# Adding a gating bias with a one-row matmul of its own, and adding the attention part last

## The reference, cut to what matters

```python
def spatial_gating(u, v, tiny, ln_g, ln_b, w_s, b_s):
    b, s, _ = v.shape
    vn = layer_norm(v, ln_g, ln_b).reshape(b, s // CHUNK, CHUNK, SGU_GROUPS, SGU_GROUP_DIM)
    mixed = jnp.einsum("gpq,bnqgc->bnpgc", w_s, vn) + b_s.T[:, :, None]
    return u * (mixed.reshape(b, s, SGU_WIDTH) + tiny)

tiny = tiny_attention(tq, tk, tv, tk_c, tv_c) @ tiny_w_o     # tiny_w_o is 64 x 1024
o_a = spatial_gating(u, v, tiny, sgu_ln_g, sgu_ln_b, sgu_w_s, sgu_b_s)
```

## Time and profile before

| | before |
|---|---|
| median of 3 runs | 2415.87 us (2413.20 to 2421.04) |
| profiled execution, its own time | 2415.87 us |
| its span, first to last instruction | 2414.1 us |
| mean granted TensorE clock | 0.933 |
| TensorE busy | 2010.9 us, 83% of the span |
| TensorE's share of the chain that ended last | 68% |
| first projection matmul of the second layer starts | 806.65 us |
| transposes of the tiny attention's output start | 971.38 us |
| gating matmuls start | 973.32 us |
| first matmul of `pe_qkv` starts | 989.60 us |

### The profile page before, as it was taken

How to read it: one execution, slowest core, us unless ns; L and a number is a source line. 1 busy time by engine, 2 the same in 40 slices (tenths; PEclk the granted TensorE clock), 3 DMA queues, 4 the chain that set the end, 5 groups by cost and what they waited for, 6 DMA issues and landing times.

```text
span 2414.1 us, 33274 instructions
## 1 busy us (share of the span) xinstructions
PE 2010.9 (83%) x13566; PEld 1361.5 (56%) x13567; DVE 923.0 (38%) x2043; ACT 552.9 (23%) x1018; POOL 401.2 (17%) x379
## 2 busy tenths in 40 slices
PE   3899989688781698996776998987999998999875
PEld 2677778454341686784444665754555555555432
DVE  2144552532214225215766122224443444434325
ACT  2132412211112214114665110020111111111111
POOL 0000000222211000001100000001444545444320
PEclk8899999699996797899999999978999999999998
DMA  6654530689993212012110122214899999999967
GB/s 258 243 227 175 210 123 12 237 338 417 417 386 134 79 53 70 18 53 79 48 48 2 61 88 104 97 53 169 350 360 357 400 404 402 365 358 395 382 247 311
DMA packets 97403, 514.79 MB, mean 213 GB/s; under 512 B 25154, under 2 KB 26210, under 8 KB 43100
## 3 DMA queue, kind: packets, MB, share of 16 engines
q1 hardware_dynamic: 62592, 449.60, 47.2%
q0 software_dynamic: 29504, 51.31, 6.0%
q10 hardware_dynamic: 5148, 11.59, 1.4%
HBM read 508.87 MB, written 49.81 MB: 231 GB/s over the span
## 4 chain that ended last, share of the span: by engine, by line
PE 68%; DVE 10%; DMA 10%; ACT 7%; issue 3%; ACTq 1%; POOL 0%; SPq 0%; DVEq 0%; POOLq 0%
PE ps L249 29%; PE ps L1689 16%; PE ps L1756 8%; DMA arena<-in_egu 7%; PE ps L1655 2%; ACT arena L2773 2%; DVE arena L2809 2%; PE ps L402 2%; DMA arena<-in_ada 2%; PE ps L1743 1%; ACT arena L2784 1%; PE ps L2758 1%; DMA arena<-y_rows 1%; PE ps L424 1%; ACT arena L267 1%
## 5 line engine op out<-in xcount | busy, mean ns | idle before, releaser
L1689 PE MATMUL ps<-arena 128*64 128x256 f32 x4096 | 479.4, 388 | 54.0 <-DMA arena<-in_egu 35.9
L1689 PEld LDWEIGHTS ps<-arena 128*64 128x64 f32 x4096 | 301.4, 140 | 256.3 <-DMA arena<-in_egu 66.2
L249 PE MATMUL ps<-arena 128*128 128x256 f32 (+4 forms) x1276 | 323.4, 416 | 2.4 <-DVE arena L491 1.3
L249 PEld LDWEIGHTS ps<-arena 128*128 128x128 f32 (+1 forms) x1276 | 229.0, 203 | 92.7 <-issue 71.2
L1756 PE MATMUL ps<-arena 128*64 128x512 f32 x1024 | 243.4, 604 | 37.0 <-issue 29.1
L1637 POOL DMA_INDIRECT arena<-h_rows,arena x160 | 193.2, 1208 | 312.6 <-DVE arena L1618 162.6
L1643 POOL DMA_INDIRECT y_rows<-arena x160 | 160.2, 1002 | 419.2 <-DVE arena L1787 369.6
L1751 DVE COPY arena<-ps 128x256 f32<-128x256 f32 (+1 forms) x96 | 36.5, 380 | 431.9 <-PE ps L1743 431.9
L1730 ACT ACTIVATE arena<-ps 128x256 f32<-128x256 f32 (+1 forms) x96 | 33.4, 348 | 503.8 <-PE ps L1689 503.8
L300 DVE TENSOR_TENSOR wlb<-arena,whb 128x1024 fp32r<-128x1024 f32 (+1 forms) x46 | 55.7, 1213 | 242.1 <-ACT whb L292 242.1
L1756 PEld LDWEIGHTS ps<-arena 128*64 128x64 f32 x1024 | 67.7, 136 | 134.7 <-issue 131.0
(11 more groups left out here) (392 smaller groups left out, 3062.2 us busy)
## 6 DMA issues: line engine op xcount, KB each, us to landing
arena<-in_egu SPq DMA_DIRECT2D x204, 1024.0 KB, 12.4
arena<-in_ed SPq DMA_DIRECT2D x102, 1024.0 KB, 8.4
arena<-in_ada SPq DMA_DIRECT2D x48, 1024.0 KB, 7.1
arena<-in_win SPq DMA_DIRECT2D x33, 1024.0 KB, 4.9
arena<-y_rows SPq DMA_DIRECT2D x20, 1024.0 KB, 13.9
arena<-in_wout SPq DMA_DIRECT2D x8, 1024.0 KB, 6.8
arena<-in_nabias POOLq DMA_DIRECT2D x16, 512.0 KB, 3.9
h_rows<-arena ACTq DMA_DIRECT2D x8, 512.0 KB, 2.9
```

What stands on the lines that cost most here:

```text
L249: z = pe.matmul(o, l, r, start=start and i == 0, stop=stop and i == len(pairs) - 1, skip_group_check=check)
L1689: z = pe.matmul(b[64 * j:64 * j + 64, 256 * s:256 * s + 256], XV[:, c, 64 * h:64 * h + 64], wk(k)[:, j * 256:j * 256 + 256], start=k == 0, ...
```

## The change

The identity rows and rows 64 to 71 of `TQ` are gone. `b_s` is loaded once as one row of 4 KB into row 0 of `BSR`. In each group a matmul of one row by 512 columns (a row of ones times the group's part of `BSR`, read four times over) opens the bank, the four mixing matmuls follow, and the 64-row matmul on `TQ` comes last, so that the wait for `totT` stands in front of it.

```diff
-                    (cut(TQ[64:72, :], 4), bc(a["bs_row"].rearrange("o (g p) -> (o g) p", g=8).unsqueeze(1), [8, 4, 128]))]
+                    (BSR[0:1, :], a["bs_row"])]
             for i, (dst, src) in enumerate(late):
                 act.dma_start(dst, src).then_inc(*l2.up("late", "late", i, by=16))
-            act.activation(cut(TWO[64:72, :], 8), bc(ident[64:72, 64:72].unsqueeze(2), [8, 8, 128]), ACT.Copy).then_inc(
-                *l2.up("act", "eight"))
...
-                w.wait_ge(*l2.to("eight"))
+                pe.matmul(cut(b.ap, 4), ones[0:1, :], bc(BSR[0:1, cols].unsqueeze(1), [1, 4, 128]), start=True, stop=False,
+                          skip_group_check=True)
+                for n in range(4):
+                    pe.matmul(b.ap[:, n * 128:(n + 1) * 128], VN[:, n, cols], WST[:, cols], start=False, stop=False,
+                              skip_group_check=True)
                 w.wait_ge(*ta.to("totT"))
-                pe.matmul(b.ap, TWO[0:72, cols], TQ[0:72, :], start=True, stop=False, skip_group_check=True)
-                for n in range(4):
-                    z = pe.matmul(b.ap[:, n * 128:(n + 1) * 128], VN[:, n, cols], WST[:, cols], start=False, stop=n == 3,
-                                  skip_group_check=True)
-                z.then_inc(*sg.up("pe", "mm", g))
+                pe.matmul(b.ap, TWO[0:64, cols], TQ[0:64, :], start=False, stop=True, skip_group_check=True).then_inc(
+                    *sg.up("pe", "mm", g))
```

## The result

The changed kernel took 2454.09 us, the median of 4 runs (2446.53 to 2457.18), against 2415.95 us before, the median of 4 (2413.20 to 2421.04). The ratio is 1.0146, 95% interval 1.0128 to 1.0166: it is 1.5% slower. Forecast was slower, by 11 us; it is 38 us, more than three times that, and 21 us above the upper end of the range. The way was right, the size was not. The profiled execution has a span of 2447.5 us, and the mean granted clock fell from 0.933 to 0.924.

A forecast was written before the change was run, and what follows sets the result against it. TensorE was taken to bound the kernel at the gating. 11.0 us there (some 6 columns, 5 row-count changes, hole included) plus 0.3 for the transfer gave +11.3 us on 2415.87: 2427.2 us, 8-in-10 range 2420 to 2433.

The forecast's parts named there:

- The bound: At the gating, TensorE bounds the kernel, running without a gap into the projection, with one hole of 1.08 us.
- Columns: In the gating, eight added one-row matmul pairs cost 0.85 us each at full clock, 6.8 us for all.
- Changes of row count: In the gating, three changes per group, each about 0.2 us at full clock and 0.30 at the lower clock.
- The disputed third change: Between groups, the step from 64 rows to 1, absent from the trace: bounds 0 and 0.20 us, taken as 0.20.
- Two changes in a group: Rival at the gating: 64 rows to 1 is free; +9.7 us, 2425.6 us; chance 0.11.
- Columns only: Rival at the gating: changes of row count cost nothing; +6.8 us with the transfer, 2422.7 us; chance 0.10.
- The sum at the gating: Group 0 at lower clock, groups 1 to 7 at full clock, 3.19 us each; projection 11.0 us later.
- What the new order covers: Before `totT`, group 0's one-row and mixing matmuls fill TensorE's only hole, giving back at most 1.08 us.
- The transfer and the collision: Front of second layer: removing `b_s` packets gains 0.2 us at most; earlier weight load delays late loads; +0.3 us taken.
- The loads collide fully: Rival at the front: late loads end 1.0 us later, clock rises later too; +13 to +14 us, 2429.5; chance 0.09.
- The late loads did not give way: Rival at the front said they would: projection up to 4.15 us sooner, +6.9 us, 2422.7 us; chance 0.06.

The follow-up runs named there:

- both128: Changed kernel with bias and tiny-attention matmuls both on 128 rows, added rows zeros; stretch from last transpose to projection 21.7 us, ratio to before 1.0010.
- warm4: Changed kernel with bias and tiny-attention matmuls on 128 rows in the first four groups, last four unchanged; stretch 25.1 us, ratio to before 1.0010.
- narrow64: Kernel before with its 72-row matmul cut to 64 rows and `b_s` left out; stretch 32.8 us, ratio to before 1.0097.
- tiny72: Changed kernel with the last matmul of each group on 72 rows instead of 64, added rows zeros; stretch 26.4 us, ratio to before 1.0063.
- block64: Kernel before with 64 rows for 72, `b_s` left out, all eight 64-row matmuls ahead of all mixing; stretch 24.2 us, ratio to before 1.0057.
- batched: Changed kernel reordered: eight bias matmuls, then all mixing, then eight tiny-attention matmuls, a bank per group; stretch 30.7 us, ratio to before 1.0035.
- dummy128row: Kernel before with one more 128-row matmul of 16 columns of zeros in each group; stretch 31.8 us, ratio to before 1.0052.
- changes4: Changed kernel with 128-row bias matmul and the 64-row matmul cut in two, first half ahead of mixing; stretch 28.3 us, ratio to before 1.0103.
- the dummies: Kernel before with one more 16-column matmul of zeros per group, on 1, 64 or 128 rows; ratios to before 1.0063, 1.0074, 1.0052.
- order72: Kernel before with only the new order, mixing first, then the 72-row matmul, identity rows kept; stretch 14.9 us, ratio to before 0.9983.
- attn72_order: Kernel before with mixing first, 72-row matmul last, and the attention's score matmuls on 72 rows instead of 64; stretch 15.4 us, ratio to before 0.9983.
- tiny128: Changed kernel with the tiny-attention matmul on 128 rows, added rows zeros, bias matmul still one row; stretch 26.3 us, ratio to before 1.0037.
- after_again: Changed kernel run once more, unchanged, against the kernel before; stretch 48.2 us, ratio to before 1.014.
- bias128: Changed kernel with the bias matmul on 128 rows, added rows zeros, tiny-attention matmul still 64 rows; stretch 25.6 us, ratio to before 1.0035.

## Why the prediction was wrong, by its steps

**The bound: right.** The gating is on the path: of the 33.4 us by which the span grew, 30.8 are there.

**Columns: right in size at full clock.** 0.85 us a pair. In both128, where nothing but the columns is added, the stretch grew by 4.3 us; eight pairs of 0.85 are 6.8, and less the hole of 1.1 and 1.1 for a rise that comes 2.1 us sooner that is 4.6.

**Changes of row count: right in size and number.** Forecast were 0.20 us at full clock and 0.30 at the lower one, three to a group. At the lower clock the group of 6.00 us is 5.12 of columns and 3 x 0.29; at full clock warm4 has 3.19 us, to the digit. The disputed third change, from 64 rows to one, costs like the others: the two between 64 and 128 rows are 0.29 each in narrow64, and at full clock the group of tiny72, with two changes, takes 3.00 us against 3.19 with three. Thus "Two changes in a group" and "Columns only" fall, and the Trainium skill's rule, in "TensorEngine Tiling (Array Packing)", Key Properties, that a change of mode drains the engine, agrees with these rows for 64 to 1 row too.

**The step that failed: the clock.** The sum at the gating let the clock rise at about 978.0, as before: it put group 0 "at the lower clock" and "Groups 1 to 7 at full clock", and gave the rise 1.5 us either way. In the changed kernel all eight groups ran at 0.50. The rise was carried over from the kernel before as if it were a matter of time since TensorE became busy. It hung on what TensorE streams (tiny72: eight rows of zeros more in one matmul of three, and the clock rose in its profile). The stretch of 8 x 6.00 us is all my own lower-clock prices; only the clock in it was wrong, and that made +30.8 out of +11.0. Half-speed groups were priced in the prediction for group 0 alone, and no rival asked what it would cost if all eight stayed there: 8 x 6.0 = 48 us could have been reckoned from the earlier trace rows. The trace of the kernel before had a sign of it, too. Ahead of the gating, from 940.4 to 972.0, TensorE was busy for 27.76 of 31.60 us, and the clock stayed at 0.50:

```profile
940.40:972.00 31.60, 27.76 (x91) 20.49 (x92) 12.72 (x28) 9.94 (x19) 0.00 (x0) 0.50 0.03 10
```

**What holds the clock down.** Shown: it isn't the columns (both128) and not the values in the added rows (zeros in both128 and tiny72). It isn't the changes of row count as such: block64 and batched stay down through 13.6 and 13.8 us without one, dummy128row has none, and changes4 has more and rose in its profile. Streams of one row or of 64 rows alone did not bring the clock up in those 13.8 and 13.6 us; the 128-row matmuls behind them did, in 4.7 and 4.3 us. The rest of the trace of the kernel before fits: ahead of each of its 28 rises TensorE ran matmuls of 72 or 128 rows, and none of fewer, for 2.4 us or more. In changes4 it rose 0.8 us into a 64-row one, behind 2.7 us of full rows.

Full rows alone are not enough, however. Before the gating in the kernel before every matmul from 959.94 on has 128 rows, and in these 12 us the clock stayed at 0.50. Many of them are short, 64 columns, and there are pauses:

```profile
959.94 1.54 PE L2541 MATMUL ps<-arena 128*128 128x128 f32 x6
961.27 2.66 PE L249 MATMUL ps<-arena 128*128 128x64 f32 x12
963.72 1.49 PE L2541 MATMUL ps<-arena 128*128 128x128 f32 x6
965.00 2.66 PE L249 MATMUL ps<-arena 128*128 128x64 f32 x12
968.11 2.82 PE L249 MATMUL ps<-arena 128*128 128x64 f32 x12 [0.45 <-DVE arena L2615]
971.38 1.06 PE L2557 MATMUL ps<-arena 128*64 128x128 f32 x4 [0.45 <-DVE arena L2615]
```

That is the same picture as in dummy128row: where the stream of full columns is broken up, by few-row matmuls, by short ones or by pauses, the clock may fail to rise. What exactly decides is open. The order of the kernels in the table isn't that of the time spent in few-row matmuls (the dummies have hardly any and stay down, tiny72 has a third and rose), nor that of the changes. That a rise also depends on how a break happens to fall in time would fit the spread of the runs of changes4 and tiny72, but nothing tests it. The changed kernel has failed to rise in both of its profiles, and its 13 runs all lie between 2446 and 2457 us.

**What the new order covers: right.** The hole was filled.

**The transfer and the collision: the mechanism right, the size near the upper bound.** Forecast was +0.3, bounds -0.2 and +1.0; measured is +0.7 in the first pair. All times that follow count from the issue of the first late load. The profiles fall into three groups by when the third weight load is issued:

| profiles | load of `b_s` | third weight load issued | projection starts, mean |
|---|---|---|---|
| before, order72, attn72_order, narrow64, block64, three dummies | 32 runs | 7.9 to 8.9 us | 9.9 to 11.0 us, 10.3 |
| both128, tiny128, tiny72, warm4 | one row | 8.4 | 9.8 to 10.8, 10.4 |
| changed, after_again, bias128, batched, changes4 | one row | 6.8 | 10.5 to 11.7, 11.2 |

In the second group ScalarE's copies of zeros stand ahead of the weight copies and push the weight load back. So the one row in place of the 32 runs is worth nothing that shows, and a weight load issued some 1.1 to 1.6 us sooner goes with a projection some 0.8 us later. The packets agree: after the weight load's first packets another 54 packets of the late loads' queue start in the changed kernel (808.7 to 812.65), and 11 in the kernel before (804.4 to 806.65). This is the collision as the prediction had it, and of its cases "The loads collide fully" comes nearest at the front. The late loads did not give way, so that rival falls.

**The rest.** The changed kernel's median is 38 us above before in the first comparison. 31.5 of it are in the two places, and 1.5 in the projection's first matmuls at the lower clock; the profiled run itself lies 5 us under the median. In the second comparison, after_again against 20 runs of the kernel before, the difference is 29.6 us. So the few microseconds that are left over lie within what two comparisons differ by.

## What to carry to other kernels

A narrow matmul (here 64 rows or one) costs its columns at the clock that it is granted, and 0.2 to 0.3 us at each change of row count. Behind a stage in which the clock was low it may also cost the higher clock for its whole stage. So price every new form of matmul at both clocks, and make the lower clock throughout a rival. Where a contraction is short, look at padding it with rows of zeros before a split: eight rows more (72 for 64) were worth 15 us of the stretch here (narrow64 against before), and with both matmuls padded to 128 rows the changed kernel can't be told from before (both128). And keep the stream of full rows and long matmuls unbroken until the clock is up; the mixed groups behind the rise held it for 12.8 us in warm4.

## What the runs showed of the hardware that was not expected

- 72 rows and 64 rows, same columns, same place: 17.4 us against 32.8 us, by the granted clock alone but for 16 changes of row count (4.6 us).
- TensorE busy without a pause for 48 us at a granted clock of 0.50.
- A pair of 16-column matmuls in each group, on 128 rows, 0.29 us each time: the clock stayed down through a stretch of 31.8 us where it rose after 4.7 us without them.
- Matmuls of 128 rows for 12 us at a granted clock of 0.50, many of them of 64 columns and with pauses (before, 959.94 to 972.24).
- Runs of one kernel 25 us apart (changes4: 2432.9 to 2458.1 us, mean clock 0.931 to 0.922). Whether the clock rises in the gating would explain it, but none of the long ones was profiled.
- A 1 MB weight load on another queue, issued 6.8 us after the first late load instead of 8.4: the projection, which waits for the late loads, starts some 0.8 us later (means of five and of four profiles).
